# Layer 0's modulation split: four tiles ahead of the first norm, eight as half tiles inside the input projection, and the small rows of each layer later

## The reference, cut to what matters

```python
mod = (jax.nn.silu(c) @ w_mod[l] + b_mod[l]).reshape(b, N_MOD, 1, d)
mod_c = (jax.nn.silu(c_ctx) @ w_mod[l] + b_mod[l]).reshape(N_MOD, 1, 1, d)
lam = diff_lambda(lam_vecs[l], lam_init)
xn = modulate(rms_norm(h, norm1_g[l]), mod[:, 0], mod[:, 1])
cn = modulate(rms_norm(hc, norm1_g[l]), mod_c[0], mod_c[1])
pc = cn @ wl            # layer 0: all columns; layer 1: k and v
p = xn @ wl
# q, k: rms norm per head, rope (tokens only); differential attention with lam;
# pool and conv branches, gates, w_out
h = h + mod[:, 2] * mix
xn2 = modulate(rms_norm(h, norm2_g[l]), mod[:, 3], mod[:, 4])
h = h + mod[:, 5] * peer_ffn(xn2, ...)   # 8 heads x 16 experts per token, rows gathered
```

## Time and profile before

| | us |
|---|---|
| runs, median (lowest to highest) | 4322.41 (4318.58 to 4325.29) |
| profiled execution, its own time | 4322.23 |
| its span | 4320.4 |
| TensorE busy | 3740.2 |
| VectorE busy | 2834.3 |
| ScalarE busy | 1160.2 |
| GpSimd busy | 903.4 |

### The profile page before, as it was taken

How to read it: one execution, slowest core, us unless ns; L and a number is a source line. 1 busy time by engine, 2 the same in 40 slices (tenths; PEclk the granted TensorE clock), 3 DMA queues, 4 the chain that set the end, 5 groups by cost and what they waited for, 6 DMA issues and landing times.

```text
span 4320.4 us, 42589 instructions
## 1 busy us (share of the span) xinstructions
PE 3740.2 (87%) x15389; PEld 2390.4 (55%) x15389; DVE 2834.3 (66%) x6599; ACT 1160.2 (27%) x2577; POOL 903.4 (21%) x772
## 2 busy tenths in 40 slices
PE   7999998788999877789896888777779989999898
PEld 3457554334745523345642555222239879898797
DVE  1442137888877788877876568886656576565764
ACT  2141011124111111231001422111124444444443
POOL 0000003433322344323331024544320000000000
PEclk7999999999999989999997999999999999999999
DMA  7273448997999999989996169999974534545343
GB/s 298 78 272 118 161 185 357 405 356 298 410 420 364 399 359 410 372 319 387 420 421 246 59 273 388 421 383 421 421 327 159 185 137 160 181 163 183 136 166 132
DMA packets 246622, 1225.90 MB, mean 284 GB/s; under 512 B 19256, under 2 KB 46202, under 8 KB 124428
## 3 DMA queue, kind: packets, MB, share of 16 engines
q0 software_dynamic: 110592, 805.36, 45.9%
q1 hardware_dynamic: 135820, 417.84, 25.9%
HBM read 1222.07 MB, written 1.05 MB: 283 GB/s over the span
## 4 chain that ended last, share of the span: by engine, by line
PE 39%; DMA 17%; DVE 16%; ACT 3%; issue 2%; POOL 1%; SPq 0%; DVEq 0%; ACTq 0%; POOLq 0%
PE ps L430 11%; DMA BIG<-in_t_uv,idx 10%; PE ps L793 7%; PE ps L794 7%; PE ps L795 7%; PE ps L768 5%; DMA gbuf<-in_t_uv,idx 4%; DVE BIG L1906 2%; DMA wbuf<-in_t_uv,idx 2%; DVE gbuf L1906 2%; DVE wbuf L1906 1%; PE ps L418 1%; DVE plo L1947 1%; DVE BIG L1899 1%; PE ps L423 1%
## 5 line engine op out<-in xcount | busy, mean ns | idle before, releaser
L430 PE MATMUL ps<-wbuf,BIG 128*128 128x512 f32 x1856 | 815.3, 596 | 15.3 <-DMA wbuf<-in_t_conv_out_w 6.6
L2722 POOL DMA_INDIRECT gbuf<-in_t_uv,idx x286 | 337.9, 1181 | 1478.8 <-DVE BIG L1819 841.7
L430 PEld LDWEIGHTS ps<-wbuf,BIG 128*128 128x128 f32 x1856 | 353.1, 192 | 448.9 <-issue 431.9
L1947 DVE TENSOR_TENSOR plo<-wbuf,phi 128x1024 fp32r<-128x1024 f32 (+1 forms) x344 | 401.6, 1180 | 286.7 <-ACT phi L1303 286.1
L768 PE MATMUL ps<-gbuf,BIG 128*128 128x512 f32 x868 | 436.1, 641 | 168.2 <-ACT BIG L1268 168.1
L768 PE MATMUL ps<-BIG 128*128 128x512 f32 x904 | 432.8, 618 | 111.0 <-ACT BIG L1268 111.0
L1283 ACT ACTIVATE BIG<-BIG 128x2 f32<-128x2 f32 x384 | 78.1, 203 | 1441.9 <-DVE BIG L1913 1439.7
L793 PE MATMUL ps<-XH,phi 128*128 128x256 f32 x1472 | 422.8, 287 | 24.6 <-DVE XL L1957 20.7
L1906 DVE CUSTOM_DVE_ANT_0 BIG<-BIG 128x1024 f32<-128x1024 f32 x292 | 355.6, 1221 | 121.3 <-DMA BIG<-in_t_uv,idx 120.7
L430 PE MATMUL ps<-BIG,wbuf 128*128 128x256 f32 (+1 forms) x2048 | 425.4, 369 | 0.5 <-DMA wbuf<-in_t_conv 0.5
L1303 ACT CAST phi<-wbuf 128x1024 fp32r<-128x1024 f32 (+1 forms) x344 | 343.8, 1013 | 292.0 <-PE ps L795 291.6
(11 more groups left out here) (359 smaller groups left out, 5072.7 us busy)
## 6 DMA issues: line engine op xcount, KB each, us to landing
wbuf<-in_t_in SPq DMA_DIRECT2D x84, 1024.0 KB, 8.6
wbuf<-in_t_w_mod SPq DMA_DIRECT2D x48, 1024.0 KB, 7.4
wbuf<-in_ffn_wg SPq DMA_DIRECT2D x20, 2048.0 KB, 7.6
wbuf<-in_ffn_wu SPq DMA_DIRECT2D x20, 2048.0 KB, 7.7
wbuf<-in_t_conv SPq DMA_DIRECT2D x48, 768.0 KB, 8.7
wbuf<-in_ffn_wd SPq DMA_DIRECT2D x16, 2048.0 KB, 7.9
wbuf<-in_t_peer_wq SPq DMA_DIRECT2D x24, 1024.0 KB, 7.1
wbuf<-in_w_in SPq DMA_DIRECT2D x14, 1536.0 KB, 6.7
```

What stands on the lines that cost most here:

```text
L430: ins = p(mm)(bank, l, r, start=(k == 0), stop=(k == 7))
L1947: v(tt)(lo, W2.of(key, rows_, n)[:, k0:k1, c0:c1], hi.bitcast(F32), ALU.subtract).then_inc(dve_piece.up(q), 1)
L2722: g(nc.gpsimd.indirect_dma_start)(slot, None, I["t_uv"], bass.IndirectOffsetOnAxis(ap=idx[:, tb % 3, j:j + 1], axis=0)).then_inc(g_landed[ ...
```

## The change

- `pe_modulation`, `act_modulation` and `dve_modulation` take a range of tiles. TensorE's step is now a half tile, not a tile; the turn of the tile before comes between the two halves; each half frees its slot by itself; the bank of a tile is held between its halves. The columns of tiles 0 to 3 and of 4 to 11 gather in two banks one after the other, and bias and `modA` are formed for each range by itself.
- Tiles 0 to 3 run ahead of the first norm as before, through `W`. Tiles 4 to 11 go through a second ring `WM` of two 1 MB slots in `BIG`, and one half runs behind each product of the projection: `pe_qkv_heads`, `act_qkv_heads` and `dve_qkv_heads` take a generator `tiles` and step it once per product.
- SP issues x and ctx before tiles 2 and 3, and the halves of tiles 4 to 11 between the projection weights.
- The angles and the layer's small rows move: VectorE and ScalarE do them behind the first four products. Squares and root of the norm come on ScalarE after two copies.
- `with_tiles` steps the tiles at each second step, as a tile has two steps now.
- For layer 1, `dve_layer_rows` and `act_layer_rows` move behind the routes in `dve_ahead` and `act_ahead`; their loads stay where they are.
- `bmod` and `sel` move within `BIG`, out of the way of `WM`.

```diff
@@ with_tiles
-        if n % 4 == 0:
+        if n % 2 == 0:
@@ build
-        bmod, sel = small_f(96), small_f(2)
+        bmod, sel = BIG[:, 24576:24672], BIG[:, 24672:24674]
+        WM = Tiles([BIG[:, i:i + 2048] for i in (20480, 22528)], [sem(f"mod_landed{i}") for i in range(2)])
@@ pe_modulation
-            for n in range(12):
+            for n in range(n0, n1):
                 key = ("mod", l, n)
                 b = ps.claim(p, key, (act_mod, (l, n)))
+                ps.held.add(ps.where[key])
                 for half in range(2):
-                    p.wait_ge(*W.landed(key + (half,)))
-                    w = W.of(key + (half,), 4, 512)
+                    p.wait_ge(*tiles.landed(key + (half,)))
+                    w = tiles.of(key + (half,), 4, 512)
                     for i in range(4):
                         ins = p(mm)(b[32 * i:32 * i + 32, :], wide_cs[:, half * 4 + i, :], w[:, i, :],
                                     start=(half == 0), stop=(half == 1))
-                ins.then_inc(pe_mod.up(l, n), 1)
-                halves_done(key, pe_mod, l, n)
-                if n:
-                    turn(n - 1)
-                yield
+                    ins.then_inc(pe_mod.up(*((l, n) if half else (l, n, "first"))), 1)
+                    tiles.done(key + (half,), pe_mod, *((l, n) if half else (l, n, "first")))
+                    if half == 0 and n > n0:
+                        turn(n - 1)
+                    yield
+                ps.held.discard(ps.where[key])
@@ pe_qkv_heads (act_qkv_heads and dve_qkv_heads step it before they take up a product)
                     if len(turns) > 1 or (turns and n >= 4):
                         turn(*turns.pop(0))
+                    next(tiles, None)
                     yield 4
@@ tensor
-            run(pe_modulation(p, 0))
+            run(pe_modulation(p, 0, 0, 4, W))
             run(pe_norm_turn(p, "A1", range(4)))
-            run(pe_qkv_heads(p, "A", "A1", 0, first, range(2), range(2)))
-            run(pe_qkv_heads(p, "A", "A1", 1, first, range(2, 6), range(4)))
+            tiles = pe_modulation(p, 0, 4, 12, WM)
+            run(pe_qkv_heads(p, "A", "A1", 0, first, range(2), range(2), tiles))
+            run(pe_qkv_heads(p, "A", "A1", 1, first, range(2, 6), range(4), tiles))
+            run(tiles)
@@ scalar
-            rows_copied = act_modulation(a, 0)
-            for _ in range(4):
+            rows_copied = act_modulation(a, 0, 0, 4)
+            for _ in range(5):
                 next(rows_copied)
             for tb in range(4):
                 act_first_squares(a, tb)
-                if tb % 2:
-                    next(rows_copied)
             turned = act_norm_turn(a, "A1", first, range(4), colA(0, 0), colB(0, 0))
             next(turned)
-            next(rows_copied)
+            run(rows_copied)
+            a.wait_ge(*dve_mod.at(0, "A", 0))
+            run(turned)
+            tiles = act_modulation(a, 0, 4, 12)
+            run(act_qkv_heads(a, "A", "A1", 0, 0, first, range(2), range(2), wide, tiles))
             for b2 in range(2):
                 act_angles(a, b2)
-                next(rows_copied)
             act_layer_rows(a, 0)
...
@@ vector
-            dve_layer_rows(v, 0, sc[:, 0:256])
-            run(dve_modulation(v, 0))
+            run(dve_modulation(v, 0, 0, 4))
...
+            run(dve_qkv_heads(v, "A", "A1", 0, 0, first, range(2), range(2), wide, tiles))
+            dve_angles(v)
+            dve_layer_rows(v, 0, sc[:, 0:256])
+            run(dve_qkv_heads(v, "A", "A1", 0, 1, first, range(2, 6), range(4), wide, tiles))
@@ dve_ahead (act_ahead likewise)
-            dve_layer_rows(v, 1, sideb.slots[0][:, 0:256])
             yield
...
             yield from routes
+            dve_layer_rows(v, 1, sideb.slots[0][:, 0:256])
             yield from scaled(dve_tokens(v), 0.8, 1)
@@ sync_start_up
             sync_modulation(s, 0, range(2))
-            sync_modulation(s, 0, range(2, 4))
             load(s, "x", H[:, 0:2, :], I["x"].rearrange("a (b p) n -> p (a b) n", p=128))
             load(s, "x", H[:, 2:4, :], I["ctx"].rearrange("a (b p) n -> p (a b) n", p=128))
-            sync_modulation(s, 0, range(4, 5))
+            sync_modulation(s, 0, range(2, 4))
...
@@ sync
             sync_qkv(s, "A", 0, 0, range(2))
-            sync_qkv(s, "A", 0, 1, range(2, 6))
+            modulation_halves(s, 4)
+            sync_qkv(s, "A", 0, 1, (2,))
+            modulation_halves(s, 5)
+            sync_qkv(s, "A", 0, 1, (3,))
+            modulation_halves(s, 6)
+            modulation_halves(s, 7)
+            sync_qkv(s, "A", 0, 1, (4,))
+            modulation_halves(s, 8)
+            modulation_halves(s, 9)
+            sync_qkv(s, "A", 0, 1, (5,))
+            modulation_halves(s, 10)
+            modulation_halves(s, 11)
```

More of the change, by code:

```diff
@@ L458, in pe_norm_turn, with pe_modulation @@
                     yield
-        def pe_modulation(p, l):
+        def pe_modulation(p, l, n0, n1, tiles):
+            cols_of = ("mod", l, n0, "cols")
             p.wait_ge(*dve_start.at("wide"))
-            held = ps.claim(p, ("mod", l, "cols"), (dve_mod, (l, "cols")))
-            ps.held.add(ps.where[("mod", l, "cols")])
+            held = ps.claim(p, cols_of, (dve_mod, (l, n0, "cols")))
+            ps.held.add(ps.where[cols_of])
             def turn(n):
@@ L481, in pe_modulation @@
                                     start=(half == 0), stop=(half == 1))
-                ins.then_inc(pe_mod.up(l, n), 1)
-                halves_done(key, pe_mod, l, n)
-                if n:
-                    turn(n - 1)
-                yield
-            turn(11)
-            ps.held.discard(ps.where[("mod", l, "cols")])
+                    ins.then_inc(pe_mod.up(*((l, n) if half else (l, n, "first"))), 1)
[4 more added lines that the diff above has]
+                ps.held.discard(ps.where[key])
+            turn(n1 - 1)
+            ps.held.discard(ps.where[cols_of])
             yield
@@ L493, in pe_gate_rows, with pe_qkv_heads @@
             b = ps.claim(p, key, (sig, event))
-            p.wait_ge(*dve_mod.at(l, "cols"))
+            p.wait_ge(*dve_mod.at(l, "modulated"))
             return turn4(p, b, [bc(modd[:, l, m, n * 4 + j, c:c + 1], [128, 128]) for j in range(4)])
-        def pe_qkv_heads(p, T, N, part, L, ns, tbs):
+        def pe_qkv_heads(p, T, N, part, L, ns, tbs, tiles=iter(())):
             turns = []
@@ L1028, in rows_gone, with act_qkv_heads @@
             e.wait_ge(*sig.at(*event))
-        def act_qkv_heads(a, T, N, l, part, L, ns, tbs, ring):
+        def act_qkv_heads(a, T, N, l, part, L, ns, tbs, ring, tiles=iter(())):
             turns = []
@@ L1453, in dve_start_up, with dve_angles @@
             v(vcopy)(posf[:, :], ps.of("pos")[:, 0:2]).then_inc(dve_start.up("pos"), 1)
+        def dve_angles(v):
             v.wait_ge(*small.at("tables"))
@@ L1513, in dve_norm_turn, with dve_modulation @@
                     ins.then_inc(dve_norm.up(N, tb, "x"), 1)
-        def dve_modulation(v, l):
-            for n in range(12):
+        def dve_modulation(v, l, n0, n1):
+            for n in range(n0, n1):
+                yield
                 yield
             yield
+            i0, i1 = n0 * 4, n1 * 4
             v.wait_ge(*small.at(("b_mod", l)))
[L1520 to L1523, removed]
+            v.wait_ge(*pe_mod.at(l, n1 - 1, "turn"))
+            v(tt)(modd[:, l, :, :, :].rearrange("p i k c -> p (i k) c")[:, i0:i1, :],
+                  ps.of(("mod", l, n0, "cols"))[:, i0 * 2:i1 * 2].rearrange("p (i c) -> p i c", c=2),
+                  bc(bmod[:, l * 48 + i0:l * 48 + i1].unsqueeze(2), [128, i1 - i0, 2]), ALU.add).then_inc(
+                      dve_mod.up(l, n0, "cols"), 1)
+            if n1 == 12:
+                dve_mod.also(l, "modulated")
             v.wait_ge(*dve_mod.now())
             for j, row in ((0, N1 + l), (1, N2 + l)):
+                if not n0 <= 6 * j + 2 < n1:
+                    continue
                 v(stt)(modA[:, l, j, :, :], modd[:, l, 3 * j + 1, :, :], 1.0, bc(cols[:, :, row:row + 1], [128, 8, 2]),
@@ L1555, in dve_rotate, with dve_qkv_heads @@
             v(tt)(dst[:, :, 1, :], m1[:, :, 1, :], m2[:, :, 0, :], ALU.add).then_inc(sig.up(*event), 1)
-        def dve_qkv_heads(v, T, N, l, part, L, ns, tbs, ring):
+        def dve_qkv_heads(v, T, N, l, part, L, ns, tbs, ring, tiles=iter(())):
             for n in ns:
                 for tb in tbs:
+                    next(tiles, None)
                     yield 4
@@ L2571, in act_ahead @@
             yield from routes
+            act_layer_rows(a, 1)
             yield from scaled(act_tokens(a), 0.8, 1)
@@ L2587, in vector @@
             next(turned)
-            dve_layer_rows(v, 0, sc[:, 0:256])
-            run(dve_modulation(v, 0))
+            run(dve_modulation(v, 0, 0, 4))
             v.wait_ge(*dve_mod.now())
             run(turned)
+            tiles = dve_modulation(v, 0, 4, 12)
```

(17 more changed lines are left out.)

16 lines of the change are left out of this document (5 added, 11 removed).

## The result

| kernel | median us | lowest to highest | runs |
|---|---|---|---|
| before | 4322.90 | 4309.66 to 4326.02 | 6 |
| changed | 4305.29 | 4302.14 to 4307.91 | 6 |

The ratio is 0.9963 (95% interval 0.9953 to 0.9974). The kernel got faster, by 17.6 us in the medians where 34 were forecast: the right direction, inside the stated range by less than 1 us, and half the size. The profiled execution took 4305.71 us, its span 4303.7.

A forecast was written before the change was run, and what follows sets the result against it. Loads bound the opening, TensorE the projection, TensorE and DMA both near their limit the attention. 4322.2 - 51.5 + 23.4 + 2 + 0 - 8 = 4288.1, forecast 4288 us; own range 4278 to 4298, whole range 4271 to 4306.

The forecast's parts named there:

- The opening: Before the projection: fewer weight halves ahead of the norm, first product at 46.6 instead of 98.06, 51.5 us removed (49 to 53).
- Eight tiles into the projection: Projection: eight modulation tiles add 23.4 us of TensorE time, and new waits on loads add 2 us.
- The waits on loads: Projection: half 5/0 waits 0.9 us behind projection weights, tiles 8 and 10 0.4 each; 2 us added.
- The tile itself: Projection: one tile by halves with its turn costs 2.92 us; eight cost 23.4, bounds 22.2 and 46.
- The reading of the bubble: Projection, after the fourth product: the 5.88 us wait stays as long, so the tile counts in full.
- The attention: Attention: layer 1's tile steps as halves; earlier issue wins up to 2 us, entries lose about as much; zero, -2 to +2.
- The late rows: Expert part, 1509 to 1525 us: VectorE's 10.29 us wait on the gains row goes; 8 us removed, 0 as low end.
- The rest: Work behind the attention, apart from the gains row: no term in the sum; the range allows a few us either way.
- B: Projection: halves late as a rule, each tile waiting one more landing of 2.48 us; 4298 to 4308 us; chance 0.12.
- C: Projection: TensorE's clock falls to 1.2 GHz and the kernel gets slower; 4369 us at half the stage; chance 0.05.
- A: Expert part: using the small rows later brings nothing, a balanced part gives the time back; 4296 us; chance 0.20.
- D: More than forecast: fast x, tiles at 2.77, the whole 10.3 us and 2 of the attention; 4281 us or lower; chance 0.13.

The follow-up runs named there:

- the second: The changed kernel run and profiled again with no edit, on another group's chip: median 4300.55 us, ratio 0.9955 to before.
- the kernel with the order mended: Changed kernel with SP issuing modulation halves ahead of the projection weights they stood behind: 4290.6 us, one time; projection 178.2 us.
- the kernel with the first two mends: Changed kernel with the turn behind the second half and SP issuing modulation halves ahead of projection weights: 4288.5 and 4288.1 us, ratios 0.9921 and 0.9922.
- the one with all three: Changed kernel with turn behind the second half, SP issuing halves first, both halves behind every second projection product: 4282.4 us, ratio 0.9915.
- whole tiles with the early turn: Changed kernel with SP issuing halves first and both halves of a tile behind every second projection product, turn still between halves: 4294.2 us, one time.
- The late turn: Changed kernel with the turn of the tile before put behind the second half, everywhere: 4287.7 us, one time; attention 82.1 us.
- the three pairs of medians: Layer 1's small rows early against late, in before, changed and mended kernels: 4320.6 and 4315.7, 4307.5 and 4305.3, 4295.8 and 4288.1 us.
- the kernel with whole tiles there: Changed kernel with layer 1's modulation beside the attention stepped by whole tiles again: 4299.0 us, ratio 0.9944; attention 86.9 us.

## Where the prediction held and where it failed

**The opening: right.** 51.5 us were to go by the first product; 53.4 did in the first profile and 49.8 in the second. x and ctx came at the faster pace: the half behind them was multiplied at 24.79, where the slower one gives 26.1 and the faster 24.5. The spread is TensorE's clock: in the first profile it was at 2.4 GHz for the last turns, in the second at 1.2. The kernel before spreads as much: with only the rows late, and the same code up to there, its first product came at 93.8 instead of 98.0, so part of the 53.4 belongs to this one pair of profiles.

**Eight tiles into the projection: mis-sized.** The terms were 23.4 + 2 = 25.4; it was 32.3. The waits on loads were put at 2 and were 5.7. Half 5/0 was there 10.3 us after SP took up the pair ahead of it at 61.96, where I had worked out 9.2, and those of tiles 8 and 10 came about 0.5 later than worked out in the same way; and the first half, of tile 4, which I had counted among those that land in time, came 2 us late. The tile itself was put at 2.92; without waits it was (178.2 - 151.7) / 8 = 3.3, and with the late turn and whole tiles (174.2 - 151.7) / 8 = 2.8. I had bounded it from above by halves at 1.2 GHz and from below by whole tiles, and then took a value from a half's own length. What I missed was outside it. In the kernel with the order mended, eight tiles with their turns take 23.2 us, as forecast; the 20 products around them take 2.6 more than in the kernel before, and the turns of q and k 0.8 more. The reading of the bubble was right: from the fourth product's end to the fifth's start it grew from 7.79 to 8.76 us, by one half tile.

A tile in pieces beside full products costs more than I allowed. The rule that I set aside, of the Trainium skill (TensorEngine Tiling, Key Properties, on the drain at a change of mode), points the same way, but a count of changes is not the whole of it. Between the kernel with the first two mends and the one with all three the changes between 32-column and full products go from four to two per tile and 2.3 us go, 0.14 us for each of 16. But whole tiles with the early turn have as many changes as halves (the turn stands between them) and saved 1.7 us all the same. And a product behind a turn, where nothing changes from 32 columns to full, takes 6.95 us, almost as long as one behind a half (6.97).

**The attention: the step that failed.** I wrote "Zero, from -2 to +2" and looked only at slots and at the entering of halves. It was +8.6. The term had no allowance for the turn, and the edit also moves the turn of the tile before from behind the whole tile to behind its first half. Beside the projection a product of 7 us lies between a tile and that turn; in the attention only one stage of 1.1 us and a half of 1.0 do, and ScalarE, which has the attention's own work first, makes the copy from 260.18 to 260.79 while the turn waits until 260.83. I had not worked out that distance for this second user. (The 3 us of loading waits that I hoped to win from were mostly those of the weight loads; the matmuls stood 0.5 us for them.) The late turn gave all of it back (82.1 us). The waits for the copy sum to 3.6 us in the changed kernel. The clock is the larger part: it stood at 0.50 from 236.9 to 247.2 us with TensorE busy for 9.0 of them, and half of that, 4.5 us, is lost. Together they are 8.1 of the 8.6. With the order mended and the early turn it stood at 0.50 for only 3.4 us (3.0 busy, 1.5 lost), the waits sum to 3.1, and the stage takes 87.3. The waits are explained by the place of the turn; why the clock fell is not, as said above. A wait of TensorE here is paid in full, because all of its attention stands behind it.

**The late rows: right at the place,** 8 forecast, 8.2 to 9.5 seen between gathers 260 and 270, 5 to 8 in two of the three pairs of medians. **The rest was put at nothing** and took 3.9 us in the first profile: 2.0 up to gather 260 and 1.9 behind the last one. No run shows why.

**The rivals.** B, halves late as a rule, was the nearest: three waits were forecast and four came, 2.9 times as long in sum, and mending the order removed them. Its time, 4298 to 4308, holds the measured one by luck all the same: the waits were 3.7 us above the forecast, not 10 or more, and the rest came from the attention and the tiles. C, the clock giving way, came true at a place I had excluded ("attention with the same halves holds 1.00") and for 3 to 10 us, not a quarter of the projection; its mechanism, waits before halves and thin products, is not shown, since the same waits left the clock alone in other kernels. A did not happen at the gathers. Of D only the fast x came. The range held only because it was drawn to 4306.

## What to carry to other kernels

When a shared helper is edited for one caller, work out the distance between producer and consumer for every caller; the same move that is free beside long products is a wait beside short ones. When work is moved behind a resource that is idle on average, the order in the single issuing queue decides, so count for each piece what stands ahead of it. Keep the pieces of foreign work together where their order is free (2 us for eight tiles here). And when the clock share of a stage has fallen, find the first instruction that ran slow before naming a wait as the cause: here it stood ahead of the waits that looked guilty.

## What the runs showed of the hardware that was not expected

TensorE's granted clock fell to 0.50 at the start of the attention behind a wait of 2.15 to 2.50 us in six profiles, and stayed at 1.00 behind such a wait in seven others: in the kernel with whole tiles there it stood at 0.50 for 8 us in which TensorE was busy 7.48. Between two executions of the changed kernel the first projection product moved from 44.6 to 48.2 us with the clock of the opening: the half behind x and ctx was multiplied at 24.79 and at 24.88, and the share from 20 to 32 us was 1.00 in one and 0.50 in the other. And the same kernel's end moved by 5 us between two profiles whose last gathers agree within 1.5.
